# The last down projection of a two-block transformer kernel on one Trainium2 core: blockwise products in the Strassen-Winograd form, seven in place of eight

## What is computed

```
h   = rmsnorm(x, norm_mlp)
hid = square(relu(h @ w_up))          # 256 x 4096
x   = x + hid @ w_down                # 4096 x 1024
out = rmsnorm(x, norm_final)
```

## Time and profile before

| | |
|---|---|
| median of three runs | 1856.82 us (1855.39 to 1857.35) |
| the profiled execution's own time | 1857.39 us |
| its span, first to last instruction | 1855.0 us |
| mean granted TensorE clock | 0.983 |
| PE busy | 1704.2 us (92%) |
| DVE busy | 492.9 us (27%) |
| down stage, first to last matmul start | 1737.2 to 1846.7 us |

### The profile page before, as it was taken

The page is one execution under the profiler, slowest core; times in us unless marked ns, Lnnn a source line. Parts: engine busy times, 40 slices in busy tenths (PEclk is TensorE's granted clock), DMA queues, the critical chain, the costliest instruction groups (busy, mean ns, idle before and its releaser), DMA issues.

```text
span 1855.0 us, 18279 instructions
## 1 busy us (share of the span) xinstructions
PE 1704.2 (92%) x7238; PEld 901.3 (49%) x7238; DVE 492.9 (27%) x993; ACT 266.5 (14%) x552; POOL 29.2 (2%) x30
## 2 busy tenths in 40 slices
PE   4999999899989899898988989978999999899998
PEld 1545686534333232332323323324767888488643
DVE  1342432332323223233232322322122211200001
ACT  2122440201010010100100001001342221000000
POOL 0110000000000000000000000001000000000000
PEclk9999999899999999999999999998999999999999
DMA  9766225499999999999999999999333234334310
GB/s 369 291 248 209 90 92 196 156 422 428 430 430 430 430 430 430 430 430 430 430 430 430 430 429 430 429 429 389 137 109 118 104 124 154 118 136 171 146 46 23
DMA packets 86887, 537.00 MB, mean 289 GB/s; under 512 B 4624, under 2 KB 5776, under 8 KB 62256
## 3 DMA queue, kind: packets, MB, share of 16 engines
q1 hardware_dynamic: 84736, 530.60, 70.5%
q10 hardware_dynamic: 2096, 5.64, 0.9%
HBM read 535.17 MB, written 1.05 MB: 289 GB/s over the span
## 4 chain that ended last, share of the span: by engine, by line
PE 70%; DMA 26%; DVE 1%; issue 1%; ACT 1%; SPq 0%; DVEq 0%; POOL 0%; POOLq 0%; ACTq 0%
PE ps L1404 33%; PE ps L1669 19%; DMA ring<-in_w_up 11%; DMA ring<-in_w_gate 9%; PE ps L1969 6%; PE ps L1657 3%; PE ps L1720 2%; DMA arena<-in_w_down 2%; DMA arena<-in_w_up 2%; DMA ring<-in_w_ada 1%; PE ps L1417 1%; PE ps L1558 1%; SPq L361 0%; PE ps L1510 0%; PE ps L1533 0%
## 5 line engine op out<-in xcount | busy, mean ns | idle before, releaser
L1669 PE MATMUL ps<-ring,arena 128*64 128x512 f32 x2304 | 512.1, 595 | 56.7 <-DMA ring<-in_w_gate 28.8
L1404 PE MATMUL ps<-arena,ring 128*128 128x256 f32 x1856 | 414.3, 383 | 2.8 <-ACT arena L712 2.5
L1404 PEld LDWEIGHTS ps<-arena,ring 128*128 128x128 f32 x1856 | 354.3, 192 | 62.7 <-issue 7.1
L1669 PEld LDWEIGHTS ps<-ring,arena 128*64 128x64 f32 x2304 | 164.1, 137 | 385.7 <-issue 317.2
L1404 PE MATMUL ps<-ring,arena 128*128 128x512 f32 (+1 forms) x480 | 197.1, 566 | 4.6 <-issue 3.4
L1669 PE MATMUL ps<-arena 128*64 128x512 f32 x768 | 174.3, 603 | 13.1 <-DMA arena<-in_w_up 10.7
L1404 PEld LDWEIGHTS ps<-ring,arena 128*128 128x128 f32 x480 | 89.7, 190 | 103.6 <-issue 99.6
L669 ACT ACTIVATE arena<-ps 128x512 f32<-128x512 f32 x32 | 19.1, 597 | 676.1 <-PE ps L1691 676.1
L1669 PEld LDWEIGHTS ps<-arena 128*64 128x64 f32 x768 | 53.4, 139 | 127.1 <-issue 108.3
L1969 PE MATMUL ps<-ring,arena 128*128 128x512 f32 x256 | 110.0, 592 | 0.0
L1720 PE MATMUL ps<-arena 128*128 128x512 f32 x128 | 69.0, 667 | 21.1 <-DVE xres L1157 19.6
(11 more groups left out here) (231 smaller groups left out, 932.2 us busy)
## 6 DMA issues: line engine op xcount, KB each, us to landing
ring<-in_w_up SPq DMA_DIRECT2D x56, 2048.0 KB, 33.8
ring<-in_w_down SPq DMA_DIRECT2D x56, 2048.0 KB, 30.7
ring<-in_w_gate SPq DMA_DIRECT2D x48, 2048.0 KB, 34.5
ring<-in_w_in SPq DMA_DIRECT2D x23, 2048.0 KB, 8.2
arena<-in_w_gate SPq DMA_DIRECT2D x16, 2048.0 KB, 29.3
arena<-in_w_up SPq DMA_DIRECT2D x16, 2048.0 KB, 28.3
arena<-in_w_down SPq DMA_DIRECT2D x16, 2048.0 KB, 35.3
ring<-in_w_ada SPq DMA_DIRECT2D x12, 2048.0 KB, 15.0
```

The lines of the kernel that those rows point to most:

```text
L1404: last = pe.matmul(dst, a, b, start=k == 0, stop=k == len(terms) - 1)
L1669: mm = pe.matmul(dst[CAP * g:CAP * g + CAP, :], stationary(half, c), w[:, c, 512 * g:512 * g + 512], start=half == 0 and c == 0, stop=half ...
```

## The change

```
+            def down_sums(i):
...
+                dve.drain()
+                dve.tensor_tensor(sa[:, 0], a21, a22, ALU.add)
+                dve.tensor_tensor(sa[:, 2], a11, a21, ALU.subtract)
+                dve.wait_ge(loaded2[j % RING], 16 * (j // RING + 1))
+                dve.tensor_tensor(t3, b22, b12, ALU.subtract)
+                dve.drain()
+                dve.tensor_tensor(b12, b12, b11, ALU.subtract)
+                dve.tensor_tensor(sa[:, 1], sa[:, 0], a11, ALU.subtract)
+                dve.drain()
+                dve.tensor_tensor(t2, b22, b12, ALU.subtract)
+                dve.tensor_tensor(sa[:, 3], a12, sa[:, 1], ALU.subtract)
+                dve.drain()
+                dve.tensor_tensor(t4, t2, b21, ALU.subtract).then_inc(sem("sums_ready"), 1)
...
+                if s in (11, 13):
+                    down_sums((s - 11) // 2)
+            for i in range(2, 8):
+                dve.wait_ge(used2, W_DOWN2 - W_QKV2 + i - 1)
+                down_sums(i)
...
+            dve.wait_ge(sem("down2_done"), 1)
+            dve.tensor_tensor(x11, p1, x11, ALU.add)
+            dve.tensor_copy(part, p1)
+            dve.drain()
+            dve.wait_ge(sem("down2_done"), 2)
+            dve.tensor_tensor(part, p6, part, ALU.add)
+            dve.drain()
+            dve.wait_ge(sem("down2_done"), 3)
+            dve.tensor_tensor(part4, p5, part, ALU.add)
+            dve.drain()
+            dve.tensor_tensor(x12, part4, x12, ALU.add)
+            dve.tensor_tensor(x22, part4, x22, ALU.add)
+            dve.wait_ge(sem("down2_done"), 4)
+            dve.tensor_tensor(part3, p7, part, ALU.add)
+            dve.drain()
+            dve.tensor_tensor(x21, part3, x21, ALU.add)
+            dve.tensor_tensor(x22, p7, x22, ALU.add)
+            dve.wait_ge(sem("down2_done"), 5)
+            dve.tensor_tensor(x11, p2, x11, ALU.add).then_inc(sem("x4_done"), 1)
+            dve.drain()
+            dve.wait_ge(sem("down2_done"), 6)
+            dve.tensor_tensor(x12, p3, x12, ALU.add).then_inc(sem("x4_done"), 1)
+            dve.wait_ge(sem("down2_done"), 7)
+            dve.tensor_tensor(x21, x21, p4, ALU.subtract).then_inc(sem("x4_done"), 2)
             dve.wait_ge(sem("nf_in"), 16)
             for tt in range(TT):
-                dve.wait_ge(sem("down2_done"), tt + 1)
-                for hh in range(2):
-                    xx = xres[:, tt, 512 * hh:512 * hh + 512]
-                    dve.tensor_tensor(xx, bank(4 + 2 * tt + hh), xx, ALU.add).then_inc(sem("x4_done"), 1)
                 dve.wait_ge(sem("ssf_done"), tt + 1)
...
+                for k, n in enumerate(P_ORDER if i < 7 else P_LAST):
+                    if k == (2 if i < 7 else 1):
+                        pe.wait_ge(sem("sums_ready"), i + 1)
+                    if i == 0 and n >= 5:
+                        pe.wait_ge(sem("up2_read"), 8 + n)
+                    for c in range(2):
+                        a, b = terms[n](c)
+                        last = pe.matmul(bank(P_BANK[n]), a, b, start=i == 0 and c == 0, stop=i == 7 and c == 1)
```

More of the change, by code:

```diff
@@ L263, in two_blocks, with quarter_sums @@
         yout = area(17408, 2048).rearrange("p (t d) -> p t d", t=TT)
+        def quarter_sums(i):
+            at = (15872, 16896, 17920, 18944) if i % 2 == 0 else (2048, 3072, 4096, 5120)
+            return (area(at[0], 1024).rearrange("p (n c q) -> p n c q", n=4, c=2),
+                    [area(a, 1024).rearrange("p (c n) -> p c n", c=2) for a in at[1:]])
+        part, part3, part4 = area(6144, 512), area(14848, 512), area(15360, 512)
+        P_BANK = (None, 4, 5, 7, 6, 0, 1, 2)
+        P_ORDER = (1, 2, 4, 3, 5, 6, 7)
+        P_LAST = (1, 6, 5, 7, 2, 3, 4)
         STICK_STEPS = 6
@@ L1360, in _ @@
             norm_out(1, "hy", V_NM2)
+            def down_sums(i):
+                j = W_DOWN2 - W_QKV2 + i
+                sa, (t2, t3, t4) = quarter_sums(i)
+                w = w4_view(W_DOWN2 + i)
+                a11, a12 = hid[:, 4 * i:4 * i + 2, 0:P], hid[:, 4 * i + 2:4 * i + 4, 0:P]
+                a21, a22 = hid[:, 4 * i:4 * i + 2, P:T], hid[:, 4 * i + 2:4 * i + 4, P:T]
+                b11, b12 = w[:, 0:2, 0:512], w[:, 0:2, 512:1024]
+                b21, b22 = w[:, 2:4, 0:512], w[:, 2:4, 512:1024]
+                dve.drain()
[11 more added lines that the diff above has]
+                dve.tensor_tensor(t4, t2, b21, ALU.subtract).then_inc(sem("sums_ready"), 1)
             for s in range(16):
@@ L1365, in _ @@
                                   relu[:, s % 2, :], ALU.mult).then_inc(sem("hid_done"), 1)
+                if s in (11, 13):
[3 more added lines that the diff above has]
+                down_sums(i)
+            x11, x12 = xres[:, 0, 0:512], xres[:, 0, 512:1024]
+            x21, x22 = xres[:, 1, 0:512], xres[:, 1, 512:1024]
+            p1, p2, p3, p4, p5, p6, p7 = (bank(b) for b in P_BANK[1:])
+            dve.wait_ge(sem("down2_done"), 1)
[22 more added lines that the diff above has]
+            dve.tensor_tensor(x21, x21, p4, ALU.subtract).then_inc(sem("x4_done"), 2)
             dve.wait_ge(sem("nf_in"), 16)
             for tt in range(TT):
-                dve.wait_ge(sem("down2_done"), tt + 1)
-                for hh in range(2):
-                    xx = xres[:, tt, 512 * hh:512 * hh + 512]
-                    dve.tensor_tensor(xx, bank(4 + 2 * tt + hh), xx, ALU.add).then_inc(sem("x4_done"), 1)
                 dve.wait_ge(sem("ssf_done"), tt + 1)
@@ L1965, in _, with hidden @@
                 w = w4_view(W_DOWN2 + i)
[L1966 to L1971, removed]
+                sa, (t2, t3, t4) = quarter_sums(i)
+                def hidden(c, tt):
+                    return hid[:, 4 * i + c, P * tt:P * tt + P]
+                terms = {
+                    1: lambda c: (hidden(c, 0), w[:, c, 0:512]),
+                    2: lambda c: (hidden(2 + c, 0), w[:, 2 + c, 0:512]),
+                    3: lambda c: (sa[:, 3, c], w[:, 2 + c, 512:1024]),
+                    4: lambda c: (hidden(2 + c, 1), t4[:, c]),
+                    5: lambda c: (sa[:, 0, c], w[:, c, 512:1024]),
+                    6: lambda c: (sa[:, 1, c], t2[:, c]),
+                    7: lambda c: (sa[:, 2, c], t3[:, c]),
+                }
+                for k, n in enumerate(P_ORDER if i < 7 else P_LAST):
[6 more added lines that the diff above has]
+                        last = pe.matmul(bank(P_BANK[n]), a, b, start=i == 0 and c == 0, stop=i == 7 and c == 1)
                         tell_used(last)
-                    if i == 7 and c == 3:
+                    if i == 7:
                         last.then_inc(sem("down2_done"), 1)
```

## The result

| | before | after |
|---|---|---|
| median of four runs | 1856.11 us (1855.02 to 1857.35) | 1841.92 us (1841.29 to 1845.23) |
| ratio, with its 95% interval | | 0.9921 (0.9909 to 0.9933) |
| the profiled execution and its span | 1857.39, 1855.0 us | 1841.82, 1839.5 us |
| down stage, first pass to the start of VectorE's last adds | 110.07 us | 96.41 us |
| from there to the end of the last scaling | 4.67 us | 4.83 us |

The ratio means 12.4 to 16.9 us less, at 0.9921 14.7. The forecast was 1843.5 us, 13.3 less.

The account below looks back on a forecast made before the run. The prediction took TensorE's passes alone to bound the down stage. Span 1855.0 - 13.73 + 0.4 = 1841.7 us; against the median, 1856.82 - 13.3 = 1843.5 us, with a range of 1841.2 to 1847.0 us, 8 times in 10.

Parts of the forecast that it names:

- The passes: Down stage on TensorE: sixteen products per weight block become fourteen, so 32 passes at 0.429 us go, 13.73 us less.
- The two prices set at zero: Down stage: two products in a row to one bank, and halves of a tile not sharing their stationary operand, cost 0.
- The satisfied waits: Down stage: eleven new semaphore waits, eight on sums and three on banks, cost nothing; upper bound 2.2 us.
- The sums: VectorE's sums, about 6.6 us a block, cost nothing under TensorE's 12.0 us per block; the first two blocks' precede the stage.
- The square behind them: Up stage: the square queued behind block 0's sums starts about 0.5 us late, and no step of that stage moves.
- The ending: After the last product: a serial VectorE chain of 5.07 us in place of 4.67, tile 0's chain now exposed, +0.4 us.
- The store: End of the span: unchanged at 3.02 us, though the first tile's store just ahead could cost up to 0.4 us.
- The sum: Whole kernel: span 1855.0 - 13.73 + 0.4 = 1841.7 us, time 1843.5 us, 0.7% less; chance 0.86.
- (1): Down stage and ending: waits, store, ending and pitch cost more than priced, 3.6 us more, 1847.1 us; chance 0.09.
- (2): Down stage: VectorE's sums become the bound, TensorE waiting from 12.3 us a block; at 15.5 us 1862.7 us; chance 0.02.
- (3): Down stage: broken passes or cycling banks drop TensorE's clock; at half clock for a quarter of it 1864 us; chance 0.03.

Follow-up runs that it names:

- e4_nosums: The changed kernel with all sums of A and B and the waits for them left out, output not the reference's; 1840.75 us, ratio 0.9916.
- e3_late: The changed kernel with the sums of blocks 0 and 1 moved from inside the loop of the squares to behind it; 1848.76 us, ratio 0.9951.
- e5_extra7: The changed kernel with one sum formed seven more times in each block, each with a drain; 1864.89 us, ratio 1.0040.

## Why the prediction was right

**The passes (13.73 us).** Measured 13.66 for the stage, from 32 passes at an unchanged 0.429 us; the missing 0.07 us lie between the last pass and its reader. The two prices set at zero, banks and stationary operands, are zero in the run that has them alone.

**The satisfied waits.** Set at zero with an upper bound of 2.2 us; they are zero, the eight for the sums by e4_nosums, the three for banks by the length of block 0.

**The sums (6.6 us a block, hidden).** Measured 6.5 us; the form with two pieces of 512 words takes 1.23 us like the others. The square behind them was 0.3 us late where I had put 0.5 (by VectorE's own timeline), and nothing moved after it. That they are hidden rests on their place, as e3_late shows, and on the condition that a block's sums take less than 12.3 us: 11.7 cost nothing, 15.6 cost 24 us. Where between the two the cost begins is only computed, not measured.

**The ending (+0.4 us).** The mechanism was right, tile 0's chain has come out from under tile 1's products, and the term was too large: +0.16 us. I added whole durations, while independent VectorE instructions overlap. The mean starts 0.60 us after the last add's start (1831.59 to 1832.19), not 0.69 plus a gap, and the second mean 1.20 us after the scaling of 1.28 (1833.07 to 1834.27). So 0.60 + 0.88 + 1.20 + 0.87 + 1.28 = 4.83 in place of 5.07. The store cost 0.06 us more, of the 0.4 allowed.

**The sum.** By stage and ending 13.4 us less, forecast 13.3. The span was 1839.5 in place of 1841.7 for a reason the sum can't hold: executions of one program reached the down stage at 1735.2 and at 1740.0 us. So the mechanism is confirmed by the stage and not by the median. The first median, 1841.92 us, lies 1.6 us below the forecast and only 0.7 above the lower end of the range, the second, 1846.46 us, 3.0 above the forecast and 0.5 below the upper end; that both fell inside is partly luck, since the range below allowed 2.3 us for variation that has been larger.

**The rivals.** (1) did not happen. (2) did not happen in the changed kernel; it is real as a mechanism and needs 2.4 times the work on VectorE: at 15.6 us a block the kernel is slower than before, 1.0040 (1.0026 to 1.0054). (3) did not happen in the changed kernel: seven banks took turns for 96 us at a granted clock of 1.00. The rule on cycling through PSUM banks ("TensorE: Matmul & The Clock Gate", section "A second HAM failure mode: psum-queue depth-cycling", in the Trainium skill), which the page tells of one bfloat16 kernel, is not borne out for this stream of float32 passes. What did bring the clock down, in e3_late and e5_extra7, were real pauses, and they came with waits for VectorE: my price for VectorE as the bound left this out, 1.8 us in e3_late and 3.1 in e5_extra7. The factor of 0.85 in the price of rival 3 was low as well: in e5_extra7, at a granted clock of 0.50 from 1842.65 to 1846.0 us, four passes took 3.78 us against 1.88, twice the time.

## What to carry to other kernels

Where TensorE is the only bound and VectorE idle, seven products in place of eight are worth an eighth of the passes, provided that the sums of one block take less than one block's passes (here 6.5 of 12.0 us) and that the sums of the first blocks lie under the stage before (here worth 6.5 us). Count the ending apart: with results spread over several banks the first tile is no longer finished early, and the order of the last products should be chosen so that one tile is. What the added sums and differences do to the rounding of the result was not measured here. Judge a change of 0.7% in the stage it touches, since executions differed by several microseconds ahead of that stage.

## What the runs showed of the hardware

- In these runs the passes behind a pause of TensorE took longer too, so that it could cost more than its length. After 4.54 us of waiting the granted clock was 0.66 and 0.50 in the next two stretches of 2 us and twelve passes took 1.8 us more; after 3.37 us, in e5_extra7, twelve passes took the same 1.8 us more; after 5.44 us twelve passes took 3.1 us more (1842.65 to 1850.95, 8.30 us in place of 5.15). Behind waits of 0.62 and 1.67 us four passes took 1.98 us, against 1.88 in the unbroken stream.
- When the clock falls around like pauses, and how long it stays down, differs between executions of one program. From 330 to 340 us the granted clock of the changed kernel was 0.98 in one profile and 0.76 in the other, and their distance grew there by 2.1 us. Behind the pause ahead of the up stage it was 0.82 and 0.55 over four microseconds, and 0.52 in the kernel before; 0.82 and 0.52 made a difference of 1.2 us in that stage.
- TensorE's pitch did not feel VectorE working at 9.28 of 10 us on the same ring and arena: 224 passes in 96.15 us with and without.
